# Fewer single blocks and one pair more in each first feed-forward layer, with part of the input sums on GpSimd

## The reference

```
h = jnp.square(jax.nn.relu(u2 @ w_ff1[l]))          # first block
x = x + gate2 * (h @ w_ff2[l])
jnp.square(jax.nn.relu(x @ w1)) @ w2                # second and third block
```

## Time and profile before

| | us |
|---|---|
| median of 3 runs (2525.19 to 2527.41) | 2525.89 |
| the profiled execution | 2524.29 |
| its span | 2522.5 |
| granted TensorE clock, mean | 0.996 |

### The profile page before, as it was taken

How to read it: one execution, slowest core, us unless ns; L and a number is a source line. 1 busy time by engine, 2 the same in 40 slices (tenths; PEclk the granted TensorE clock), 3 DMA queues, 4 the chain that set the end, 5 groups by cost and what they waited for, 6 DMA issues and landing times.

```text
span 2522.5 us, 38409 instructions
## 1 busy us (share of the span) xinstructions
PE 2471.1 (98%) x15181; PEld 2144.2 (85%) x15181; DVE 1699.1 (67%) x3249; ACT 1294.5 (51%) x2558; POOL 404.4 (16%) x476
## 2 busy tenths in 40 slices
PE   7999999999999999999999999999999999999998
PEld 6876677899988978778897999889898887999888
DVE  5476977688863499997774988535635744987533
ACT  4365554367742435564654687424534453677422
POOL 2233342200000156553000100000000100100000
PEclk9999999999999999999999999999999999999999
DMA  9532234434443233223421333332321442333332
GB/s 285 136 93 71 63 101 121 132 99 126 118 126 98 80 101 94 58 67 95 131 84 51 92 111 108 96 96 82 93 76 34 134 126 59 85 111 107 93 99 86
DMA packets 455092, 253.29 MB, mean 100 GB/s; under 512 B 16458, under 2 KB 449310, under 8 KB 454911
## 3 DMA queue, kind: packets, MB, share of 16 engines
q1 hardware_dynamic: 451615, 243.18, 33.7%
q0 software_dynamic: 3152, 7.59, 1.2%
q10 hardware_dynamic: 144, 0.07, 0.0%
HBM read 247.99 MB, written 2.80 MB: 99 GB/s over the span
## 4 chain that ended last, share of the span: by engine, by line
PE 84%; DVE 10%; ACT 3%; issue 2%; DMA 1%; SPq 0%; POOL 0%; DVEq 0%; ACTq 0%; POOLq 0%
PE ps L1134 15%; PE ps L1136 15%; PE ps L1142 15%; PE ps L1199 4%; PE ps L1201 4%; PE ps L1204 4%; PE ps L1049 4%; PE ps L1051 4%; PE ps L1047 4%; PE ps L1375 2%; PE ps L1232 1%; DVE ps L3034 1%; PE ps L1229 1%; PE ps L1227 1%; PE ps L1720 1%
## 5 line engine op out<-in xcount | busy, mean ns | idle before, releaser
L1950 ACT ACTIVATE wh<-w_f 128x512 fp32r<-128x512 f32 (+2 forms) x621 | 351.1, 614 | 337.7 <-PE ps L1142 158.1
L2914 DVE TENSOR_TENSOR w_r<-w_f,wh 128x512 fp32r<-128x512 f32 (+1 forms) x459 | 295.9, 688 | 334.1 <-ACT wh L1950 333.6
L1134 PE MATMUL ps<-XH,wh 128*128 128x512 f32 (+1 forms) x1136 | 458.0, 403 | 4.4 <-ACT wh L1950 3.5
L1136 PE MATMUL ps<-XL,wh 128*128 128x512 f32 (+2 forms) x1016 | 398.0, 392 | 0.2 <-DVE XL L3434 0.2
L1142 PE MATMUL ps<-XH,w_r 128*128 128x512 f32 (+2 forms) x1160 | 309.2, 390 | 1.1 <-DVE w_r L2914 0.8
L1136 PE MATMUL ps<-arena_r,wh 128*128 128x512 f32 (+1 forms) x808 | 297.1, 373 | 0.1
L4213 POOL TENSOR_TENSOR w_r<-w_f,wh 128x256 fp32r<-128x256 f32 (+1 forms) x314 | 236.1, 782 | 352.2 <-ACT wh L1950 352.2
L1134 PEld LDWEIGHTS ps<-XH,wh 128*128 128x128 f32 (+1 forms) x1136 | 211.9, 186 | 69.2 <-issue 16.0
L1142 PEld LDWEIGHTS ps<-XH,w_r 128*128 128x128 f32 (+2 forms) x1160 | 215.5, 186 | 51.2 <-DVE w_r L2914 3.2
L1136 PEld LDWEIGHTS ps<-XL,wh 128*128 128x128 f32 (+2 forms) x1016 | 189.5, 186 | 42.8 <-issue 1.7
L1134 PE MATMUL ps<-arena_r,wh 128*128 128x512 f32 (+1 forms) x568 | 210.6, 379 | 0.8 <-ACT wh L1950 0.8
(11 more groups left out here) (499 smaller groups left out, 5913.4 us busy)
## 6 DMA issues: line engine op xcount, KB each, us to landing
w_f<-in_mlp_w SPq DMA_DIRECT2D x126, 512.0 KB, 4.0
w_f<-in_w_ff SPq DMA_DIRECT2D x63, 512.0 KB, 4.1
w_f<-in_w_in SPq DMA_DIRECT2D x49, 512.0 KB, 3.9
w_f<-in_ada_w SPq DMA_DIRECT2D x35, 512.0 KB, 4.0
w_f<-in_even_w_in SPq DMA_DIRECT2D x35, 512.0 KB, 3.8
w_f<-in_odd_w_in SPq DMA_DIRECT2D x23, 512.0 KB, 3.7
w_f<-in_even_w_out SPq DMA_DIRECT2D x16, 512.0 KB, 3.9
w_f<-in_xa_w_v SPq DMA_DIRECT2D x16, 512.0 KB, 3.3
```

The costliest lines, as they stand in the source:

```text
L1134: e.matmul(b, hi[:, k, :], xh, start=u.first and k == 0, stop=False)
L1136: e.matmul(b, hi[:, k, :], xl, start=False, stop=False)
L1950: e.activation(high_flat(u)[:, s], flat(u, 0)[:, s], ACT.Copy).then_inc(act.sem, act.up("high", u.n, i))
L2914: e.tensor_tensor(low[:, s], raw_[:, s], high[:, s], ALU.subtract).then_inc(dve.sem, dve.up("low", u.n, i))
```

## The change

`SINGLES` is 1, so each stage has 14 pairs. The single gets a slot of its own for its high part (index 6, in the arena where the last product slot was); the four product slots are three slots of the ring, free since the tail of the layer before, and the single's. Sums 5 and 7 are made by GpSimd as soon as their chunks are normalized (chunk 3 of the second half for sum 5, chunk 7 for sum 7), sums 6 and 4 by VectorE behind the single's low pieces; the low parts of sums 5 and 4 by GpSimd, those of 6 and 7 by VectorE in turns 3 and 5 of its product loop. ScalarE makes high part 5 ahead of its first turn, the lead's relus and high part 6 in turn 2, high parts 7 and 4 in turn 3, the single's relu in turn 4. VectorE's squares of the lead come in turn 10. GpSimd's two squares follow its low parts. The first pair's order is 1, 2, 5, 6, 3, 7. The late columns move one pair back. Lines that stay are left out below but for a few that say where one is.

```diff
...
-SINGLES = 3
+SINGLES = 1
+FIRST_PRODUCTS = (1, 2, 5, 6, 3, 7)
+POOL_LOWS = (5, 4)
-ADA_AFTER = {1: 0, 4: 1, 7: 2, 10: 3}
+ADA_AFTER = {2: 0, 5: 1, 8: 2, 11: 3}
...
-        order += [(j, PRODUCTS[0])] + ([(j - 1, 4)] if j else []) + [(j, p) for p in PRODUCTS[1:]]
+        order += [(j, PRODUCTS[0])] + ([(j - 1, 4)] if j else []) + [(j, p) for p in (PRODUCTS if j else FIRST_PRODUCTS)[1:]]
...
     def mlp(stage, w1, w2, x):
-        plans[stage, "ff1"][-1].high = HIGH_SLOTS
+        plans[stage, "ff1"][-1].high = HIGH_SLOTS + LEAD
...
-        for n, u in zip((0, 1, 2), plans[stage, "ff2"][0:1] + [u for u in plans[stage, "ff2"][1:] if u.name != "ada"][:2]):
+        for n, u in zip((0, 2, 3), plans[stage, "ff2"][0:1] + [u for u in plans[stage, "ff2"][1:] if u.name != "ada"][:2]):
...
         def product_slot(st, i):
-            u, v, w_ = plans[st, "ff1"][0], plans[st, "ff1"][1], plans[st, "ff2"][0]
-            a = {0: high_slots[u.high], 1: high_slots[v.high], 3: high_slots[w_.high]}.get(i % PRODUCT_SLOTS)
-            a = last_slot if a is None else a[:, HALF_SHIFT:HALF_SHIFT + 2 * QUARTER * WC]
+            u = slot_heirs[st][i % PRODUCT_SLOTS]
+            a = high_slots[u.high]
+            a = a if u.high == HIGH_SLOTS + LEAD else a[:, HALF_SHIFT:HALF_SHIFT + 2 * QUARTER * WC]
-        last_slot = area(O_PRODUCT, 2 * QUARTER * WC, r=True)[0]
+        high_slots.append(area(O_PRODUCT, 2 * QUARTER * WC, r=True)[0])
+        slot_heirs = []
+        for st in range(3):
+            single, (a, b, c) = plans[st, "ff1"][0], [u for u in units if u.high_after and u.high_after[1] == st]
+            slot_heirs.append((b, c, a, single))
         def ada_sums(st):
...
-            if i < 2:
-                return pe, "unit", plans[st, "ff1"][i].n
-            return pe, "unit", plans[(st, "ff1"), "lead"][0].n
+            if i == PRODUCT_SLOTS - 1:
+                return pe, "unit", plans[st, "ff1"][0].n
+            return pe, "unit", slot_heirs[st][i].high_before.n
         def pair_of(st, j):
...
-                        w.wait_ge(dve, "sum low", st, p)
+                        w.wait_ge(pool if p in POOL_LOWS else dve, "sum low", st, p)
                     begins = p in (1, 2, 5)
...
-            def sums_high(st, source, bias=None):
-                for n, p in enumerate((5, 6, 7, 4)):
-                    t, high = sums[n][:, 1, :, :], sums_r[n][:, 0, :, :]
-                    w.wait_ge(dve, "sum", st, p)
-                    if p in NO_BIAS:
-                        e.activation(high, t, ACT.Copy).then_inc(act.sem, act.up("sum high", st, p))
-                    else:
-                        for k in range(QUARTER):
-                            c = bias(k + QUARTER) if p == BIAS else bias_step[:, k:k + 1]
-                            e.activation(high[:, k, :], t[:, k, :], ACT.Identity, bias=c, scale=1.0).then_inc(
-                                act.sem, act.up("sum high", st, p))
-            def block_products(st, single, late):
+            def sum_high(st, p, bias):
+                n = (5, 6, 7, 4).index(p)
+                t, high = sums[n][:, 1, :, :], sums_r[n][:, 0, :, :]
+                w.wait_ge(pool if p in (5, 7) else dve, "sum", st, p)
+                if p == 7:
+                    w.wait_ge(dve, "bias step", st)
+                if p in NO_BIAS:
+                    e.activation(high, t, ACT.Copy).then_inc(act.sem, act.up("sum high", st, p))
+                else:
+                    for k in range(QUARTER):
+                        c = bias(k + QUARTER) if p == BIAS else bias_step[:, k:k + 1]
+                        e.activation(high[:, k, :], t[:, k, :], ACT.Identity, bias=c, scale=1.0).then_inc(
+                            act.sem, act.up("sum high", st, p))
+            def block_products(st, early, late):
...
                 for i in range(len(order) + PRODUCT_SLOTS):
-                    if i == PRODUCT_SLOTS:
-                        run_steps([single])
+                    early(i)
...
             def mlp(st, column, bias=None):
-                run(((st, "ff1"), "lead"))
-                run_steps(plans[st, "ff1"][:1])
-                sums_high(st, None, column)
-                run_steps(plans[st, "ff1"][1:-1])
                 def rest(n=2):
...
+                def early(i):
+                    if i == 0:
+                        sum_high(st, 5, column)
+                    elif i == 2:
+                        run(((st, "ff1"), "lead"))
+                        sum_high(st, 6, column)
+                    elif i == 3:
+                        sum_high(st, 7, column)
+                        sum_high(st, 4, column)
+                    elif i == PRODUCT_SLOTS:
+                        run((st, "ff1"))
                 def late(i):
-                    if bias and biases and i % 6 == 0 and i < -8:
+                    if bias and biases and i % 6 == 0 and PRODUCT_SLOTS - len(order) <= i < -8:
-                block_products(st, plans[st, "ff1"][-1], late)
+                block_products(st, early, late)
...
-                e.tensor_tensor(t[5], b12, b11, ALU.subtract).then_inc(dve.sem, dve.up("sum", st, 5))
-                e.tensor_tensor(t[7], b22, b12, ALU.subtract).then_inc(dve.sem, dve.up())
-                w.wait_ge(dve, "sum", st, 5)
+                w.wait_ge(pool, "sum", st, 5)
-                dve.marks["sum", st, 7] = dve.count
-            def sums_low(st, bias):
-                for n, p in enumerate((5, 6, 7, 4)):
-                    t, low, high = sums[n][:, 1, :, :], sums_r[n][:, 1, :, :], sums_r[n][:, 0, :, :].bitcast(F32)
-                    w.wait_ge(act, "sum high", st, p)
-                    if p == 6:
-                        w.wait_ge(dve, "sum", st, 4)
-                    if p in NO_BIAS:
-                        e.tensor_tensor(low, t, high, ALU.subtract).then_inc(dve.sem, dve.up("sum low", st, p))
-                    else:
-                        for k in range(QUARTER):
-                            c = bias(k + QUARTER) if p == BIAS else bias_step[:, k:k + 1]
-                            e.scalar_tensor_tensor(out=low[:, k, :], in0=t[:, k, :], scalar=c, in1=high[:, k, :],
-                                                   op0=ALU.add, op1=ALU.subtract).then_inc(dve.sem, dve.up("sum low", st, p))
-            def block_products(st, late):
+            def sum_low(st, p, bias):
+                n = (5, 6, 7, 4).index(p)
+                t, low, high = sums[n][:, 1, :, :], sums_r[n][:, 1, :, :], sums_r[n][:, 0, :, :].bitcast(F32)
+                w.wait_ge(act, "sum high", st, p)
+                if p == 6:
+                    w.wait_ge(dve, "sum", st, 4)
+                for k in range(QUARTER):
+                    c = bias(k + QUARTER) if p == BIAS else bias_step[:, k:k + 1]
+                    e.scalar_tensor_tensor(out=low[:, k, :], in0=t[:, k, :], scalar=c, in1=high[:, k, :],
+                                           op0=ALU.add, op1=ALU.subtract).then_inc(dve.sem, dve.up("sum low", st, p))
+            def block_products(st, early, late):
...
                 for i in range(len(order) + PRODUCT_SLOTS):
+                    early(i)
...
             def mlp(st, source, columns_):
-                run_steps(lead)
-                run_steps(plans[st, "ff1"][:1])
-                sums_low(st, lambda k: columns_(k, 1))
-                run_steps(plans[st, "ff1"][1:])
                 def rest(n=2):
...
+                def early(i):
+                    p = {3: 6, 5: 7}.get(i)
+                    if p:
+                        sum_low(st, p, lambda k: columns_(k, 1))
+                    if i == 10:
+                        run_steps(lead)
+                        run((st, "ff1"))
                 def late(i):
-                block_products(st, late)
+                block_products(st, early, late)
...
             def run(stage):
+            def input_sums(st, source):
+                t = {p: sums[n][:, 1, :, :] for n, p in enumerate((5, 6, 7, 4))}
+                b11, b12, b22 = source[:, near, HALVES[0]], source[:, near, HALVES[1]], source[:, far, HALVES[1]]
+                for p, x, y, k in ((5, b12, b11, QUARTER - 1), (7, b22, b12, KC - 1)):
+                    if st == 0:
+                        w.wait_ge(dve, "scaled", 1, k, 1)
+                    else:
+                        w.wait_ge(dve, "norm", (st, 1), k)
+                    e.tensor_tensor(t[p], x, y, ALU.subtract).then_inc(pool.sem, pool.up("sum", st, p))
+                for p in POOL_LOWS:
+                    n = (5, 6, 7, 4).index(p)
+                    if p == 5:
+                        w.wait_ge(dve, "sum", st, 6)
+                    w.wait_ge(act, "sum high", st, p)
+                    e.tensor_tensor(sums_r[n][:, 1, :, :], t[p], sums_r[n][:, 0, :, :].bitcast(F32), ALU.subtract).then_inc(
+                        pool.sem, pool.up("sum low", st, p))
...
+            input_sums(0, mlp_in)
             run(((0, "ff1"), "lead"))
...
```

(1 more changed line is left out.)

## The result

The changed kernel takes 2547.39 us (median of four runs, 2546.10 to 2551.34) against 2525.57 us for the kernel before; the ratio is 1.0095 with a 95% interval of 1.0079 to 1.0112, 21.8 us slower. Forecast were 2552.6 us, in a range of 2536 to 2560. The profiled execution took 2546.99 us.

The account below looks back on a forecast made before the run. TensorE, busy 98%, was taken as the bound, VectorE just behind. Stage losses of 6.6, 9.7 and 9.8 us plus 0.2 each gave +26.7 on 2524.29: 2551.0, and 1.6 more for the median, 2552.6 us; range 2536 to 2560.

Parts of the forecast that it names:

- The front: Delay of each stage's eighth product against the earlier first product: +6.6, +9.7 and +9.8 us in the three stages.
- VectorE's own 17.6 us: VectorE's own list from the end of the input's low parts to the eighth product: 3.7 plus 13.9 us.
- 10.5 us of turns: GpSimd stopping VectorE ahead of the eighth product: four 128x1024 instructions at 2.2 us and two squares at 0.85, each stage.
- The price of a turn: Stop of VectorE by one GpSimd instruction over 128x1024: 2.2 us, twice the stop of a 512-wide one.
- the squares' 1.7: GpSimd's two squares ahead of the eighth product stop VectorE 0.85 us each.
- The single's start 3 us late: After the lead, GpSimd's sum 7 between the input's low parts makes the single block start about 3 us late.
- Rival 1: GpSimd runs beside VectorE without stopping it: 2523.4 us, or 2526.8 with the squares still stopping VectorE; chance 0.08.
- Rival 2: GpSimd's stops of VectorE are half as long: 10.5 us slower in all, 2536.4 us; chance 0.10 for +5 to +18.
- Rival 3: Clock falls after TensorE's waits: hidden at the fourth product, not at the eighth; three of those +5, 2557.7 us; chance 0.12.
- Rival 4: The change is harmless: the saved 1.0 us a stage arrives in full and more, 2522 us at best; chance 0.02.
- The place of the first turn: GpSimd's sum 5 stops VectorE about 2.2 us inside the second half's normalization or centring, in all three stages.
- at an unchanged 1.42 us: TensorE's 98 products a stage keep their pitch of 1.42 us each.

Follow-up runs that it names:

- four columns: The changed kernel with GpSimd's four instructions cut from 128x1024 to 128x4, part of the computation left out; 2528.29 us against 2522.63 for the kernel before.
- sums made twice: The changed kernel with each of GpSimd's two sums made twice in a row, nothing left out; 2562.12 us against 2522.63 for the kernel before.
- squares late: Changed kernel with GpSimd's sums and low parts back on VectorE, and GpSimd's two squares held until the fifteenth product low part; 2536.48 us against 2524.05 before.
- one input: The changed kernel with GpSimd's four instructions reading one SBUF tensor instead of two, part of the computation left out; 2535.33 us against 2524.05 for the kernel before.
- everything on VectorE: The changed kernel with sums 5 and 7 and low parts 5 and 4 back on VectorE, GpSimd keeping two squares; 2537.59 us against 2522.63 before.
- sum 5 late: The changed kernel with GpSimd's sum 5 started after the whole normalization, not its first half; 2547.86 us against 2546.82 for the changed kernel.

## Why the prediction was right, and where it was not

**The front, right.** VectorE's own 17.6 us plus 10.5 us of turns gave +6.6, +9.7 and +9.8 us at the eighth product, plus 0.2 a stage. Measured: +6.7, +9.7, +9.8. A small part of this fit is luck: the turns came to 10.2 us, not the 10.5 of the sum, so the rest of the way took 0.3 to 0.4 us more than its 17.6. The two errors cancelled. The price of a turn, taken as 2.2 from the 512-wide one, is 2.13 (four columns, and sums made twice), the squares' 1.7 is 1.66 (squares late). The single's start 3 us late is 3.1 in the second stage (11.80 us from the lead's second half against 8.72 in the earlier trace rows).

**Rival 1, GpSimd beside VectorE: wrong.** Its price without the new stops, but with the squares', was -1.0, +0.9 and +1.0 us in the three stages; the four columns showed -0.2, +1.2 and +1.3, in the first stage with the wait for ScalarE that the price left out.

**Rival 2, half-sized stops: wrong** for these instructions: all four were whole. With one input a stop was a third of it (0.76).

**Rival 3, the clock: half right.** The wait of 4.3 us before the fourth product was followed by a fall in all stages, and it is hidden, as said, since VectorE sets the eighth product. Windows, in the second stage and the third:

```profile
1454.40:1459.00 4.60, 4.60 (x22) 0.52 0.32 88
```

```profile
2219.50:2223.50 4.00, 4.00 (x22) 0.57 0.21 53
```

It also ate the second wait: 2.4 us were forecast before the eighth product, 0.3 to 1.4 were left, because TensorE arrived late by itself. No fall followed them in the changed kernel. In other runs one did: with everything on VectorE, TensorE waited 2.33 us before the eighth product, and then 4.6 us ran at the 1.2 GHz level, on the path and outside the fronts of the table:

```profile
1456.40:1461.00 4.60, 4.60 (x21) 0.50 0.31 93
```

So the unhidden fall of this rival does occur, though not behind every such wait: with one input, the third stage waited 2.06 us there and kept a granted clock of 1.00.

**Rival 4, harmless: wrong.** It had 2522 us at best.

**The place of the first turn, wrong in one stage.** I had sum 5 stop VectorE inside the normalization in all three stages, "even inside a run of VectorE without a gap". In the first stage it asked in such a run and got nothing for 5.8 us. GpSimd, then VectorE:

```profile
531.35 8.14 POOL L4303 TENSOR_TENSOR arena_f<-arena_f 128x1024 f32<-128x1024 f32 x1 [47.21 <-DVE arena_f L3478]
```

```profile
532.76 3.26 DVE L3485 SCALAR_TENSOR_TENSOR XL<-arena_f,modc,XH 128x256 fp32r<-128x256 f32 x8
535.93 1.30 DVE L2929 TENSOR_TENSOR w_r<-w_f,arena_r 128x512 fp32r<-128x512 f32 x2
537.13 2.38 DVE L3494 TENSOR_TENSOR soft<-modc 128x4 f32<-128x4 f32 x1
```

The stop comes at 537.1, at the same 128x4 instruction as with sum 5 late. The changed kernel's second trace, sums made twice and one input have the same 5.8 us in this stage. Why GpSimd is let in at once in the other stages isn't shown. It changed nothing in the sum, which goes by the number of turns. The Trainium skill, SBUF — State Buffer, section "Who interferes with whom", has the engine that issues first keep the ports for its instruction. The stops of 2.1 us agree, those of 0.8 us by one-input instructions of 2.7 us don't, and by this trace a run of VectorE can keep GpSimd out for far longer than one instruction.

**The term that was off: products "at an unchanged 1.42 us".** The forecast was 4 us too high for the profiled execution (2551.0 against 2546.99). From the eighth product to the last, against the first to the last before, the stages took 0.4, 0.5 and 4.8 us less: the third stage ran at 113 ns a matmul instead of 118, 1.36 us a product. Outside the three layers the execution lost 2.2 us more: 2.0 less ahead of the first layer, 2.8 more between the first and the second, 1.4 more between the second and the third. So 5.7 us came off by this term, and 2.2 us came on that no term stood for. The 2.8 arises in a stretch of low clock in code that didn't change; the windows of the same place after and before:

```profile
1244.00:1250.50 6.50, 5.83 (x14) 0.50 0.00 0
```

```profile
1239.00:1245.00 6.00, 5.23 (x24) 1.00 0.09 28
```

The changed kernel's second trace has the second and third stage at 113 too, but not the 2.8 (732.43 us between the layers, 732.41 before). 26.3 - 5.7 + 2.2 = 22.8 us is the difference of the spans. The medians' 21.8 us fit the same reading: the front's 26.3, less 4.4 for the pitch of one later stage (113 ns in both stages of both traces after, in one of two in both traces before). The medians themselves have no trace, so this is argued, not shown.

## What to carry to other kernels

Work that VectorE and GpSimd both do from two tensors in SBUF is not divided between them: on a path that VectorE sets, a GpSimd instruction over 128x1024 cost twice (2.13 us) what VectorE needs for the same (1.1 us). Before work is taken from the cover of a bound engine (here two singles, 10.9 us of cover for 1.0 us saved a stage; that alone cost 13.8 us in all), add up the second engine's list ahead of the first point where it is awaited; that sum came out within 0.1 us a stage here. Read a difference of some microseconds from traces, between two fixed instructions, not from totals: the changed kernel's front repeated within 0.1 us while its times ran from 2541.49 to 2551.34 us.

## What the runs showed of the hardware that was not expected

- Two pitches of the 128x256 matmuls with a new weight load each, 113 and 118 ns, at a granted clock of 1.00; a stage can keep one for up to 129 us, and the same program takes either in the same stage.
- A run of VectorE without a pause ran at full speed for 5.8 us beside a GpSimd instruction whose span had begun, and only then was stopped, in the first stage of four traces alike.
- The stop of VectorE by GpSimd over 128x1024 is 2.13 us with two inputs and 0.76 with one, though GpSimd's own record is 2.4 and 2.8 us; cut into 128x256 it is 0.50 each.
